# Conv layer: sums beside the taps, one row pipeline up to the output projection, and that projection with rows outermost

## The chip, the cores and the metric

The kernel runs on one core of a Trainium2 chip. The metric is the time of one execution on the device in microseconds, the median of several runs. The engines are TensorE (PE, its weight loads PEld), VectorE (DVE), ScalarE (ACT), GpSimd (POOL) and SyncE (SP), which issues the transfers of the weights.

## What is computed

The kernel is a stack of layers on 512 tokens of 1024 features. The change is in one of them, the conv layer, whose core in the reference is this (E_WIDTH 2048, 31 taps, rows of 64 tokens; the tokens are eight such rows):

```python
def _layernorm(x, g, b):
    xf = x.astype(jnp.float32)
    xc = xf - jnp.mean(xf, axis=-1, keepdims=True)
    var = jnp.mean(xc * xc, axis=-1, keepdims=True)
    return (xc * lax.rsqrt(var + EPS) * g.astype(jnp.float32) + b.astype(jnp.float32)).astype(x.dtype)

def _conv_mixer(h, w_in, b_in, dw, dw_b, ln_g, ln_b, w_out, b_out, conv_fn):
    p = h @ w_in + b_in
    a, gl, gate = jnp.split(p, 3, axis=-1)
    u = a * jax.nn.sigmoid(gl)
    u = conv_fn(u, dw, dw_b)
    u = jax.nn.silu(_layernorm(u, ln_g, ln_b))
    return (u * jax.nn.silu(gate)) @ w_out + b_out
```

The result, times a gate of the modulation, is added to x. All is float32.

## The kernel before

Everything is kept features first: a row is 128 features (on the partitions) by 512 tokens, so the 2048 features of the conv layer are 16 rows, in the tile Y. The program is a list of blocks; at the end of a block all engines meet. Within a block each engine runs its own list in order and they wait on counting semaphores. Weights come as tiles of 2 MB, 128 by 4096, into two slots of K.W; SP issues tile i + 2 when tile i is used up (`prefetch`, line 347).

**Input projection and taps** (`conv_layer`, first block). 12 tiles: 8 of kind G, which hold two value rows (j = 0, 1) and the two rows of their sigmoid gates (j = 2, 3), and 4 of kind Z, the outer gate, in the order GGGZGGZGGZGZ. PE makes four products of eight plain float32 matmuls a tile (line 2884), each into its own bank; tiles alternate between banks 0 to 3 and 4 to 7. ACT applies the sigmoid to j = 2, 3 of a G tile (line 2899) and silu to the four of a Z tile (2905). For each G tile, group g, DVE evacuates the two values (2926), multiplies them with the sigmoids (2932) and then runs 31 taps on each of the two rows (2943, 2947), the two rows in turn, each tap waiting for the one before on its row. Behind the products PE adds up the 16 rows with a matrix of ones (2890), as they come out of the taps.

**Layer norm** (`layer_stats`, second block). DVE takes the mean (2826) and subtracts it from each row (2830), ACT squares (2837), PE sums the squares (2821), ACT makes rstd with Ln and Exp (2840, 2843).

**Scale, silu, gate** (third block). DVE scales 16 rows (2961), ACT applies silu behind it (2974), and then DVE multiplies 16 rows by the outer gate (2966).

**Output projection** (fourth block: `linear_deep`, `Deep`, `Feed`). A float32 product is made of three fp32r products: operands are split into a high part and the rest, and hi*hi, lo*hi and hi*lo are added up. ACT makes high parts of weights (`make_hi`, 518) and rows (`Feed.high`, 396), DVE the rest (527, 406). A weight part is 8 blocks of 128 x 128: one output block j by eight rows. So `split_products` (539) makes 24 matmuls into one bank for each part. Two parts fit in K.parts. The loops are: four tiles, a pair for each half of the outputs (m), the two of a pair (kg) being the two halves of the 16 input rows; in each, four output blocks. All 16 rows are split first, and DVE takes a bank (2788) when its second product is done.

`token_products` (785) in other layers is a product with three matmuls into each of four banks in turn, 24 in all. `Ada.rows` (2057) uses matmuls with 32 columns of weights.

## Time and profile before

| | us |
|---|---|
| median of 3 runs | 4752.32 (4749.88 to 4752.86) |
| profiled execution, its own time | 4745.9 |
| its span | 4743.2 |
| PE busy | 4386.6 (92%) |
| DVE busy | 2499.2 (53%) |
| ACT busy | 1609.2 (34%) |
| granted clock of PE over the span | 0.96 |

The sums below are made against the profiled execution; times in them are microseconds from the start of the span. The conv layer's block with the taps begins at 2732, its output projection ends at 3213. In the timeline a row gives start, length, engine, line, operation and tiles, the number of instructions merged, and in brackets how long the engine was idle before and what ended that. A granted clock of 1.00 is 2.4 GHz, one of 0.5 is 1.2 GHz.

### The profile page before, as it was taken

Reading aid. Unit: us, or ns where it says so; the run is one execution under the profiler, and the core shown is the slowest. Engines: PE = TensorE matmul, PEld = TensorE weight load, DVE = VectorE, ACT = ScalarE, POOL = GpSimd, SP = SyncE. Lnnn points to the kernel's source line nnn. Section 1 sums busy time; section 2 is a strip of 40 time slices with the busy share of each in tenths; the row PEclk is TensorE's granted clock in tenths of the full one; section 3 lists DMA queues with packets and bytes.
Section 4 is the critical chain, followed back from the end, with each engine's and each line's share of the span. In section 5 each row is a group of like instructions: output and inputs, shape, how many; then the busy total and the mean of one; then the engine's idle time right before and its main releaser. Section 6 shows DMA issues by size and latency. Waiting matters only on the chain. (4 is left out here: it accounts for less than half of the span.)

```text
span 4743.2 us, 78502 instructions
## 1 busy us (share of the span) xinstructions
PE 4386.6 (92%) x31788; PEld 3326.4 (70%) x31788; DVE 2499.2 (53%) x4059; ACT 1609.2 (34%) x2467; POOL 320.6 (7%) x307
## 2 busy tenths in 40 slices
PE   8898999999999989999998899978998999999987
PEld 7665787676688767888887644456877567666675
DVE  3635543434445331777777379944534355555563
ACT  2324322323322232666665210133222233334332
POOL 0120000000000000111111000000000022221220
PEclk9889999998999999999999999989998999999998
DMA  3201222221122232111111312111221210000101
GB/s 146 108 19 71 89 98 102 78 82 71 71 89 99 100 129 84 55 59 51 59 54 35 142 55 87 71 54 71 107 98 71 105 37 21 21 20 20 55 3 54
DMA packets 36642, 337.18 MB, mean 71 GB/s; under 512 B 4081, under 2 KB 6385, under 8 KB 18545
## 3 DMA queue, kind: packets, MB, share of 16 engines
q1 hardware_dynamic: 36336, 332.76, 19.0%
q8 instruction: 235, 3.85, 0.3%
q14 instruction: 71, 0.57, 0.0%
HBM read 320.16 MB, written 12.58 MB: 70 GB/s over the span
## 5 line engine op out<-in xcount | busy, mean ns | idle before, releaser
L539 PE MATMUL ps<-hi,weight_parts 128*128 128x512 f32 x5136 | 1610.3, 394 | 121.7 <-DVE lo L406 76.7
L539 PEld LDWEIGHTS ps<-hi,weight_parts 128*128 128x128 f32 x5136 | 979.3, 191 | 341.5 <-issue 123.1
L539 PE MATMUL ps<-lo,weight_parts 128*128 128x512 f32 x2568 | 1011.3, 394 | 0.0
L527 DVE TENSOR_TENSOR weight_parts<-w,weight_parts 128x1024 fp32r<-128x1024 f32 (+1 forms) x336 | 407.0, 1213 | 968.0 <-ACT weight_parts L518 967.8
L518 ACT ACTIVATE weight_parts<-w 128x1024 fp32r<-128x1024 f32 (+1 forms) x336 | 352.0, 1049 | 1200.3 <-PE ps L539 996.5
L539 PEld LDWEIGHTS ps<-lo,weight_parts 128*128 128x128 f32 x2568 | 490.1, 191 | 102.2
L3527 PEld LDWEIGHTS ps<-buffers 64*64 64x64 f32 x12544 | 422.3, 136 | 135.0 <-issue 132.8
L3527 PE MATMUL ps<-buffers 64*64 64x64 f32 x12544 | 450.1, 226 | 61.7 <-issue 33.5
L2409 PE MATMUL ps<-x_parts,column_parts 128*128 128x512 f32 x1536 | 360.6, 392 | 10.4 <-DVE column_parts L2643 9.9
L2884 PE MATMUL ps<-x,w 128*128 128x512 f32 x768 | 331.6, 595 | 6.8 <-PEq L815 6.8
L2409 PEld LDWEIGHTS ps<-x_parts,column_parts 128*128 128x128 f32 x1536 | 286.6, 189 | 69.8 <-DVE column_parts L2643 10.3
L2947 DVE SCALAR_TENSOR_TENSOR buffers<-buffers,vecs 128x392 f32<-128x392 f32 (+14 forms) x480 | 287.0, 716 | 0.0
L2884 PEld LDWEIGHTS ps<-x,w 128*128 128x128 f32 x768 | 146.5, 191 | 191.2 <-issue 191.2
L3520 PE MATMUL ps<-h,w 128*128 128x512 f32 x512 | 228.4, 600 | 1.2 <-PEq L3351 1.2
L3520 PEld LDWEIGHTS ps<-h,w 128*128 128x128 f32 x512 | 96.2, 191 | 117.1 <-issue 115.7
L2434 PE MATMUL ps<-h 128*128 128x128 f32 x1024 | 129.4, 281 | 35.1 <-DVE w L2687 22.6
L2434 PEld LDWEIGHTS ps<-h 128*128 128x128 f32 x1024 | 124.5, 195 | 42.5 <-DVE w L2687 22.2
L3781 ACT ACTIVATE buffers<-ps 128x256 f32<-128x256 f32 x160 | 61.3, 383 | 179.6 <-PE ps L3527 173.9
L3508 POOL TENSOR_TENSOR buffers<-buffers,const 128x512 f32<-128x512 f32 x80 | 101.5, 1269 | 273.9 <-PE ps L3527 204.0
L2643 DVE TENSOR_TENSOR column_parts<-w,column_parts 128x1024 fp32r<-128x1024 f32 x64 | 78.7, 1230 | 58.1 <-ACT column_parts L2515 58.1
L2623 POOL MEMSET w<- 128x1024 f32 x1 | 1.0, 951 | 1539.6 <-POOLq L2130 1539.6
L2409 PE MATMUL ps<-context_parts,column_parts 128*128 128x256 f32 x768 | 104.0, 292 | 0.0
(481 smaller groups left out, 5336.5 us busy)
## 6 DMA issues: line engine op xcount, KB each, us to landing
w<-in_weights SPq DMA_DIRECT2D x126, 2048.0 KB, 8.0
w<-in_wh SPq DMA_DIRECT2D x64, 512.0 KB, 3.6
v_kept<-buffers SPq DMA_DIRECT2D x4, 1024.0 KB, 5.2
buffers<-v_kept SPq DMA_DIRECT2D x16, 256.0 KB, 2.6
h<-x_kept SPq DMA_DIRECT2D x2, 2048.0 KB, 10.4
x<-in_xT SPq DMA_DIRECT2D x4, 512.0 KB, 11.0
x_kept<-h SPq DMA_DIRECT2D x1, 2048.0 KB, 6.9
vc_kept<-x SPq DMA_DIRECT2D x4, 512.0 KB, 2.6
```

The costliest lines, as they stand in the source:

```text
L518: act.activation(K.parts[:, j % 2, 0, 0:nk, :], part_of(K, slot, j, nk, by_row), ACT.Copy)\
L527: dve.tensor_tensor(K.parts[:, j % 2, 1, 0:nk, :], part_of(K, slot, j, nk, by_row), K.parts[:, j % 2, 0, 0:nk, :].bitcast(F32), ALU.subtra ...
L539: mm = pe.matmul(ps, K.parts[:, j % 2, m, k, :], x[:, k * T:(k + 1) * T], start=(first and k == 0 and n == 0), stop=(last and k == nk - 1 ...
L2409: mm = pe.matmul(o, parts[:, half, w, k, :], src[:, m, k, 0:width], start=(k == 0 and n == 0), stop=(k == 7 and n == 2), skip_group_check= ...
L2434: mm = pe.matmul(bank[:, s], l[:, s], r[:, s], start=True, stop=True)
L2643: dve.tensor_tensor(half[:, 1], weight(name), half[:, 0].bitcast(F32), ALU.subtract).then_inc(DL.step(name), 1)
L2884: mm = pe.matmul(bank(i, j), w[:, k, j * P:(j + 1) * P], K.H[:, k, :], start=(k == 0), stop=(k == 7))
L2947: dve.scalar_tensor_tensor(y, u, w, y, ALU.mult, ALU.add).then_inc(K.sem("tapped"), 1)
L3508: pool.tensor_tensor(C, AS, on_chunks(f"{'clow' if d == 0 else 'cup'}{l}"), ALU.mult).then_inc(GM.step(f"c{l}"), 1)
L3520: mm = pe.matmul(K.ps[:, 2 + m % 2, :], w[:, k, m * P:(m + 1) * P], K.H[:, k, :], start=(k == 0), stop=(k == 7))
L3527: mm = pe.matmul(dst[hr(h)], lhsT[hr(h)], rhs[hr(h)], start=start, stop=stop, skip_group_check=True)
L3781: act.activation(in_half(T1, half), bank_half(0, half), ACT.Copy)\
```

## The change

1. The first G tile. PE's order of products in a G tile is 0, 2, 1, 3. For group 0, DVE evacuates value 0, multiplies by gate 0 and runs 19 taps of row 0; only then come value 1, gate 1 and the taps of row 1, in turn with the 12 left of row 0, then 19 of row 1 alone. The other groups are as before: both values, both gates, taps in turn.
2. Sums beside the taps. ACT squares each row as it leaves the taps, into 16 tiles (12 of a new buffer, and sq, ln, rstd): groups 0 to 6 right behind the last sigmoid, group 7 at the end. PE adds up rows and squares, each sum over 32 columns of ones into its own quarter of one bank. The block `layer_stats` is gone.
3. `conv_out` is one block from the sums to the end. Two matmuls over half of the partitions fold the sums to mean and moment; the variance is moment less mean squared, at least 0. Then each row goes through centring, scaling, silu, gating and splitting in turn.
4. The projection (`Outer`) runs over rows outermost: the weights are laid out by rows (`by_rows`), a part is one input row by all eight output blocks, and all eight banks are accumulated at once. The split rows stand in rings of four. A weight part is made when the row two before it is multiplied.

```diff
@@ def tiles_conv(a):
-    return [next(of[kind]) for kind in CONV_TILES] + deep(a["conv_w_out_2"][0])
+    return [next(of[kind]) for kind in CONV_TILES] + by_rows(a["conv_w_out_2"][0])
+class Outer:
+    RING = 4
+    def sync(self, sp):
+        K = self.K
+        prefetch(K, sp, self.nk // 4, lambda g: sp.wait_ge(K.sem("lo_made"), K.count("lo_made", 4 * (g + 1))))
+    def weights_high(self, act, k):
+        K = self.K
+        make_hi(K, act, by_row=True)(k // 4, 0, k // 4, (K.tile + k // 4) % 2, k % 4)
+    def high(self, act, k, row):
+        K = self.K
+        act.wait_ge(K.sem("product"), K.count("product", k - self.RING + 1))
+        act.activation(self.hi[:, k % self.RING, :], row, ACT.Copy).then_inc(K.sem("x_hi"), 1)
+    def low(self, dve, k, row):
+        K = self.K
+        dve.wait_ge(K.sem("x_hi"), K.count("x_hi", k + 1))
+        dve.tensor_tensor(self.lo[:, k % self.RING, :], row, self.hi[:, k % self.RING, :].bitcast(F32), ALU.subtract)\
+           .then_inc(K.sem("x_lo"), 1)
+    def tensor(self, pe, free=None):
+        K = self.K
+        for k in range(self.nk):
+            pe.wait_ge(K.sem("lo_made"), K.count("lo_made", k + 1))
+            pe.wait_ge(K.sem("x_lo"), K.count("x_lo", k + 1))
+            hi, lo = self.hi[:, k % self.RING, :], self.lo[:, k % self.RING, :]
+            for o in range(8):
+                if k == 0 and free is not None:
+                    free(o)
+                for n, (m, x) in enumerate(((0, hi), (0, lo), (1, hi))):
+                    mm = pe.matmul(K.ps[:, o, :], K.parts[:, k % 2, m, o, :], x, start=(k == 0 and n == 0),
+                                   stop=(k == self.nk - 1 and n == 2), skip_group_check=True)
+                if k == self.nk - 1:
+                    mm.then_inc(K.sem("outputs"), 1)
+            if k < self.nk - 1:
+                mm.then_inc(K.sem("product"), 1)
+    def take(self, dve):
+        K = self.K
+        for o in range(8):
+            dve.wait_ge(K.sem("outputs"), K.count("outputs", o + 1))
+            self.add(dve, o // 4, o % 4, K.ps[:, o, :])
@@ def conv_layer(K):
+    order_of = lambda i: (0, 2, 1, 3) if CONV_TILES[i] == "G" else (0, 1, 2, 3)
+    alone = 19
+    first_taps = [(0, n) for n in range(alone)]
+    for n in range(31):
+        first_taps += [(1, n)] + [(0, n + alone)] * (n + alone < 31)
...
-            for k in range(16):
-                pe.wait_ge(K.sem("tapped"), K.count("tapped", 62 * (k // 2) + 61 + k % 2))
-                pe.matmul(sum_bank, K.c("ones"), Y[:, k * T:(k + 1) * T], start=(k == 0), stop=(k == 15))
+            for g in range(8):
+                pe.wait_ge(K.sem("square"), K.count("square", 2 * g + 2))
+                for n, a in enumerate((tile(Y, 2 * g), tile(Y, 2 * g + 1), squares[2 * g], squares[2 * g + 1])):
+                    pe.matmul(sum_bank[32 * n:32 * n + 32], K.c("ones")[:, 0:32], a, start=(g == 0), stop=(g == 7),
+                              skip_group_check=True)
...
+            def square(g):
+                act.wait_ge(K.sem("tapped"), K.count("tapped", 62 * g + 62))
+                for k in (2 * g, 2 * g + 1):
+                    act.activation(squares[k], tile(Y, k), ACT.Square).then_inc(K.sem("square"), 1)
...
+                if i == at[7]:
+                    for g in range(7):
+                        square(g)
+            square(7)
@@ def conv_out(K, Y, Zg, mean, folded, sum_at, add):
+        def _(act):
+            act.activation(folded, K.ps[:, sum_at, :], ACT.Copy).then_inc(K.sem("step_act"), 1)
+            outer.weights_high(act, 0)
+            act.preload_act_table_set(LN_EXP)
+            act.wait_ge(K.sem("mean"), K.count("mean", 1))
+            act.activation(K.sq[:, 0, :], mean, ACT.Square).then_inc(K.sem("moment"), 1)
+            act.wait_ge(K.sem("variance"), K.count("variance", 2))
+            act.activation(K.ln[:, :], K.sq[:, 1, :], ACT.Ln, bias=K.c("eps")).then_inc(K.sem("logged"), 1)
+            act.wait_ge(K.sem("logged"), K.count("logged", 1))
+            act.activation(K.rstd[:, :], K.ln[:, :], ACT.Exp, scale=-0.5).then_inc(K.sem("rstd"), 1)
+            act.preload_act_table(ACT.Silu)
+            outer.weights_high(act, 1)
...
+            silu(0)
+            for k in range(16):
+                if k < 15:
+                    silu(k + 1)
+                act.wait_ge(K.sem("gated"), K.count("gated", k + 1))
+                outer.high(act, k, row(Y, k))
+                if 0 < k < 15:
+                    outer.weights_high(act, k + 1)
...
+            outer.weights_low(dve, 0)
+            dve.wait_ge(K.sem("summed"), K.count("summed", 1))
+            dve.tensor_scalar(mean, mean_ps, 1.0 / count, None, ALU.mult).then_inc(K.sem("mean"), 1)
+            dve.wait_ge(K.sem("mean"), K.count("mean", 1))
+            center(0)
+            dve.wait_ge(K.sem("moment"), K.count("moment", 1))
+            dve.wait_ge(K.sem("summed"), K.count("summed", 2))
+            dve.scalar_tensor_tensor(K.sq[:, 1, :], moment_ps, 1.0 / count, K.sq[:, 0, :], ALU.mult, ALU.subtract)\
+               .then_inc(K.sem("variance"), 1)
+            dve.wait_ge(K.sem("variance"), K.count("variance", 1))
+            dve.tensor_scalar(K.sq[:, 1, :], K.sq[:, 1, :], 0.0, None, ALU.max).then_inc(K.sem("variance"), 1)
+            center(1)
+            dve.wait_ge(K.sem("rstd"), K.count("rstd", 1))
+            scale(0)
+            outer.weights_low(dve, 1)
+            for k in range(16):
+                if k < 15:
+                    scale(k + 1)
+                dve.wait_ge(K.sem("silu"), K.count("silu", k + 1))
+                dve.tensor_tensor(row(Y, k), row(Y, k), row(Zg, k), ALU.mult).then_inc(K.sem("gated"), 1)
+                if k < 14:
+                    center(k + 2)
+                outer.low(dve, k, row(Y, k))
+                if 0 < k < 15:
+                    outer.weights_low(dve, k + 1)
+            outer.take(dve)
```

## Rows read from the trace of the kernel before

**Rows 1.** The page's header: span of the profiled execution.

```profile
span 4743.2 us, 78502 instructions
```

**Rows 2.** Windows: stretch, length, busy PE, PEld, DVE, ACT, POOL, clock, DMA, GB/s.

```profile
2764.00:3074.00 310.00, 310.00 (x724) 137.28 (x723) 309.79 (x522) 29.59 (x37) 0.00 (x0) 1.00 0.21 81
...
3063.50:3077.80 14.30, 14.29 (x34) 6.04 (x32) 11.21 (x20) 0.69 (x1) 0.00 (x0) 1.00 0.39 147
...
3123.00:3128.60 5.60, 5.60 (x13) 4.47 (x14) 5.60 (x9) 5.60 (x11) 0.00 (x0) 0.51 0.00 0
3128.60:3212.95 84.35, 84.31 (x372) 69.44 (x370) 26.21 (x29) 16.41 (x17) 0.00 (x0) 1.00 0.27 100
```

**Rows 3.** Timeline, DVE and ScalarE, first and last group of the taps: start, length.

```profile
2748.23 0.75 DVE L2926 TENSOR_SCALAR buffers<-ps,vecs 128x512 f32<-128x512 f32 x1 [6.12 <-PE ps L2884]
...
2763.29 1.00 DVE L2943 TENSOR_SCALAR buffers<-buffers,vecs 128x512 f32<-128x512 f32 x2
...
3037.35 0.69 DVE L2932 TENSOR_TENSOR buffers<-buffers 128x512 f32<-128x512 f32 x1 [0.21 <-ACT buffers L2899]
...
3038.87 35.84 DVE L2947 SCALAR_TENSOR_TENSOR buffers<-buffers,vecs 128x392 f32<-128x392 f32 x60
...
3036.63 0.69 ACT L2899 ACTIVATE buffers<-ps,vecs 128x512 f32<-128x512 f32 x1 [4.84 <-PE ps L2884]
```

**Rows 4.** Timeline from the last sums to the output projection's end.

```profile
3063.89 13.90 PE L2890 MATMUL ps<-buffers,const 128*128 128x512 f32 x32
...
3078.09 0.69 DVE L2826 TENSOR_SCALAR buffers<-ps 128x512 f32<-128x512 f32 x1 [3.38 <-PEq L2867]
...
3079.54 1.23 ACT L2837 ACTIVATE sq<-buffers 128x512 f32<-128x512 f32 x2 [14.76 <-DVE buffers L2830]
...
3097.19 0.69 ACT L2840 ACTIVATE ln<-ps,const 128x512 f32<-128x512 f32 x1
3097.91 0.63 ACT L2843 ACTIVATE rstd<-ln 128x512 f32<-128x512 f32 x1
3098.79 1.28 ACT L2970 ACT_TABLE_LOAD   x1 [0.26 <-PEq L2816]
3099.15 10.69 DVE L2961 SCALAR_TENSOR_TENSOR buffers<-buffers,vecs,rstd 128x512 f32 x16 [10.62 <-PEq L2816]
3100.09 10.63 ACT L2974 ACTIVATE buffers<-buffers,vecs  x16
3109.76 9.72 DVE L2966 TENSOR_TENSOR buffers<-buffers  x16
...
3122.16 2.49 DVE L406 TENSOR_TENSOR lo<-buffers,hi 128x512 fp32r<-128x512 f32 x4
...
3123.00 0.77 PE L539 MATMUL ps<-hi,weight_parts 128*128 128x512 f32 x1 [25.95 <-DVE lo L406]
...
3212.95 0.75 DVE L2788 SCALAR_TENSOR_TENSOR h<-ps,mod,h 128x512 f32<-128x512 f32 x1 [4.69 <-PE ps L539]
```

**Rows 5.** Timeline of the projection's weight parts, and a chained pair on DVE.

```profile
3131.41 1.06 ACT L518 ACTIVATE weight_parts<-w 128x1024 fp32r<-128x1024 f32 x1 [1.26 <-PE ps L539]
...
3136.85 1.06 ACT L518 ACTIVATE weight_parts<-w 128x1024 fp32r<-128x1024 f32 x1 [4.38 <-PE ps L539]
...
3137.95 1.23 DVE L527 TENSOR_TENSOR weight_parts<-w,weight_parts 128x1024 fp32r<-128x1024 f32 x1 [3.79 <-ACT weight_parts L518]
...
3724.46 0.48 DVE L3334 TENSOR_SCALAR buffers<-buffers,small 128x512 f32<-128x512 f32 x1
...
3724.97 0.75 DVE L3336 SCALAR_TENSOR_TENSOR buffers<-buffers,vecs 128x511 f32<-128x511 f32 x1
```

**Rows 6.** Timeline: 32-column passes (L2057), and ScalarE waiting for L785's products.

```profile
2710.59 3.64 PE L2057 MATMUL ps<-w,ada_in 128*32 128x512 f32 x32 [1.74 <-PEq L2095]
...
3722.22 1.06 ACT L3263 ACTIVATE weight_parts<-w 128x1024 fp32r<-128x1024 f32 x1 [4.38 <-PE ps L785]
...
3727.66 1.06 ACT L3263 ACTIVATE weight_parts<-w 128x1024 fp32r<-128x1024 f32 x1 [4.38 <-PE ps L785]
```

More of the change, by code:

```diff
@@ L2950, in _ @@
                 one(g)
-    K.done(product=48, taken_dve=16, taken_act=16, taken_gate=16, glu=16, tapped=62 * 8, step_dve=1)
+    K.done(product=48, taken_dve=16, taken_act=16, taken_gate=16, glu=16, tapped=62 * 8, step_dve=1, square=16)
     K.tile += 12
-    layer_stats(K, Y, 16, 2048.0, K.c("eps"), K.big(32 * T, T), sum_bank)
-    g, b = K.v("conv_ln_g"), K.v("conv_ln_b")
-    with nc.Block() as block:
+    K.shut()
+    conv_out(K, Y, Zg, tile(U[:, 0, :], 0), tile(U[:, 0, :], 1), sum_at, gated_plus_x(K, m, 0))
@@ new lines, in conv_layer, with conv_out, _, taken @@
+    K.shut()
+    K.shut()
+def conv_out(K, Y, Zg, mean, folded, sum_at, add):
+    nc = K.nc
+    g, b = K.v("conv_ln_g"), K.v("conv_ln_b")
+    row = lambda a, k: a[:, k * T:(k + 1) * T]
+    count = 32 * 2048.0
+    mean_ps, moment_ps = K.ps[:, sum_at + 1, :], K.ps[:, sum_at + 2, :]
+    with Outer(K, 16, add) as outer, nc.Block() as block:
+        @block.sync
+        def _(sp):
+            outer.sync(sp)
+        @block.tensor
+        def _(pe):
+            pe.wait_ge(K.sem("step_act"), K.count("step_act", 1))
+            for half, ps in ((slice(0, 64), mean_ps), (slice(64, 128), moment_ps)):
+                pe.matmul(ps, K.c("ones")[half], folded[half], start=True, stop=True).then_inc(K.sem("summed"), 1)
+            def taken(o):
+                pe.wait_ge(K.sem("variance"), K.count("variance", 1))
+                pe.wait_ge(K.sem("mean"), K.count("mean", 1))
+            outer.tensor(pe, taken)
+        @block.scalar
+        def _(act):
[10 more added lines that the diff above has]
+            outer.weights_high(act, 1)
+            def silu(k):
+                act.wait_ge(K.sem("scaled"), K.count("scaled", k + 1))
+                act.activation(row(Y, k), row(Y, k), ACT.Silu, bias=b[:, k:k + 1]).then_inc(K.sem("silu"), 1)
+            silu(0)
[6 more added lines that the diff above has]
+                    outer.weights_high(act, k + 1)
@@ L2969, in _, with center @@
-        def _(act):
-            act.preload_act_table(ACT.Silu)
-            with act.Fori(0, 16) as i:
-                at = Y[:, ds(i * T, T)]
-                act.wait_ge(K.sem("scaled"), K.count("scaled", i + 1))
-                act.activation(at, at, ACT.Silu, bias=b[:, ds(i, 1)]).then_inc(K.sem("silu"), 1)
-    K.done(scaled=16, silu=16)
-    K.shut()
-    with Parts(K, 16) as (hi, lo):
-        linear_deep(K, hi, lo, 8, gated_plus_x(K, m, 0), feed=Feed(K, tiles_of(Y, 16), hi, lo))
-    K.shut()
+            def center(k):
+                dve.tensor_tensor(row(Y, k), row(Y, k), mean, ALU.subtract).then_inc(K.sem("centered"), 1)
@@ L2982, in sgu_layer @@
+            outer.take(dve)
+        outer.done()
+    K.done(step_act=1, summed=2, mean=1, moment=1, variance=2, logged=1, rstd=1, silu=16, scaled=16, gated=16, centered=16)
 def sgu_layer(K):
```

113 lines of the change are left out of this document (57 added, 56 removed).

## Prediction

> **What bounds the kernel now.** The page gives the span [rows 1] and shows TensorE busy nearly everywhere, so I did not read it for a bound of the whole. I looked up the lines of the conv layer in the timeline and cut its 480 us into stretches. Three stretches have different limits.
>
> First the taps: in 310 us both PE and DVE are busy throughout [rows 2]. Which of the two sets the end is settled by one row: for group 7, the last one, DVE has evacuated its values and then waits 0.21 us for the last sigmoid, which ScalarE started at 3036.63 behind a product of PE [rows 3]. PE's input projection runs without a gap at 6.87 us for a product of eight matmuls (DVE, which waits for each, starts at 2748.23 after a wait of 6.12 behind its 0.75). So PE's 44th product starts the last group of taps, and then DVE needs 35.8 us.
>
> Second, from the last tap (3038.87 + 35.84 = 3074.71) to the first product of the output projection (3123.00): 48.3 us in which one pass over 16 rows follows the next: sums, mean and centring, squares and their sums, rstd, scaling with silu, gating, and only then the split [rows 4]. PE is nearly idle for 25 of them. This is the stretch that the change attacks.
>
> Third, the output projection: 384 matmuls, the first 5.6 us at a granted clock of 0.51, the rest at 1.00 [rows 2], the last bank taken at 3212.95 [rows 4]. It takes 89.95 us from first matmul to last take; a product of 24 matmuls takes 5.44 us (3131.41 to 3136.85) [rows 5]. PE sets the pace there.
>
> **Part 1, the first tile reordered.** In the new order (value 0, gate 0, value 1, gate 1) the sigmoid of channel block 0 can follow the second product, done at 2748.2, rather than the third [rows 3]. With the table load (1.28), the sigmoid and the multiply (0.69 each) the first tap would start at about 2750.9 instead of 2763.3, 12.4 us earlier. Against that, 19 taps of block 0 and later 19 of block 1 run alone, each waiting for the one before. Now 60 taps take 35.84 us, 0.60 each, because two chains alternate; a chained instruction starts about 0.04 us behind the end of the other (3724.46 + 0.48 to 3724.97) [rows 5]. At a middle length of 0.72 us, my estimate from the neighbouring 0.75 us row, that is some 0.75 each: 38 x 0.15 = 6 us. So DVE ends group 0 about 6 us earlier. But what is late next? The last group still cannot start its taps before the sigmoid that ends at 3037.32, since both gates precede the taps there and the fourth product of a tile stays the fourth. The lead is spent in that wait: it grows from 0.21 to about 6 us. PE's pace depends on none of this, as the banks of tile 0 are wanted back only when tile 2 starts, four products behind 2761.8, at about 2789. I count 0.2 us at most, take 0, and keep the full 6 us as a rival.
>
> **Part 2, sums beside the taps.** The 16 squares move to ScalarE. Fourteen run behind the last sigmoid (from 3037.3, 14 x 0.6 = 8.6 us, as two take 1.23 [rows 4]), ahead of the last four gates, whose first product PE ends one product of 6.87 us behind the sigmoid's, at 3043.5. That delays the first gates by 2 to 3 us, and nobody waits for these. Only the last two squares are exposed: 0.03 + 1.2 us behind the last tap, 3075.95. PE then does four sums of 32 columns side by side. The nearest row is the 128*32 group, 32 passes in 3.64 us, 0.11 each [rows 6]: eight passes 0.9 us, or 1.8 at half clock, plus about 0.3 of start and drain. PE has been idle for 6 us by then (28 of 32 sums are done from 3063.5 on in some 6 us); behind its longer gap today it starts at half clock [rows 2], so I lean to that end. Today PE's 16 full sums take 13.9 us [rows 4] and end at 3077.79, and the block's end costs 0.30 to 3078.09. New: block end at 3077.5 to 3078.4, I take 3078.2. Part 2 alone saves nothing here; its worth is that the pass of squares in the block that follows, from 3079.54 to the Ln at 3097.19, disappears.
>
> **Part 3, from the sums to the first product.** I lay the written order out from that block end, with the durations of [rows 4] and [rows 5] and 0.03 to 0.04 us for a handoff. ScalarE copies the sum (0.69), splits weights (1.06): 1.69. DVE's low half (1.15 until the next may start) lies in front of the mean: 2.88; this covers PE's two small sums. Mean 0.69: 3.60. Square of it 0.63: 4.26. Variance 0.75: 5.04. Clamp 0.48: 5.55. Ln 0.69: 6.27. Exp 0.63: 6.93. Silu's table 1.28: 8.24. Second weight part 1.06 on ScalarE: 9.3, and 1.15 on DVE: 10.45. Scaling of row 1 (0.67 until the next): 11.12. Gate of row 0, 0.69: 11.8. Its high part, behind silu of row 1: 12.5. Low part 0.69: 13.2. PE 0.15 later (low part ends 3122.85, PE at 3123.00): 13.4. So PE starts at 3078.2 + 13.4 = 3091.6 instead of 3123.00: 31.4 us. The bounds: 2 us less if the moment sum lies hidden and PE is at full clock, 3 us more if each of the 15 steps costs 0.2 us of handoff.
>
> The table load is on that chain once. In the trace 1.28 us are followed by the activation 0.02 us later [rows 4]. The Trainium skill, page "ScalarE: Activation LUTs", section "What ACT_TABLE_LOAD costs", counts a drain of about 1.38 us beside each load; by it the start would be some 1.4 us later, and the rows here don't show it.
>
> **Part 4, rows outermost.** The matmuls are as many and of the same form; PE's 89.95 us stay if it is fed. Eight banks are accumulated at once and the bank changes every three matmuls. The nearest rows are those of L785, where the bank changes every three matmuls too: ScalarE, which waits for its products of 24, starts at 3722.22 and 3727.66, 5.44 us apart as well [rows 6]. What is new is that in each row the work of the feeding engines hangs on PE: weight part k+1 may be made only when row k-1 has been multiplied, and ScalarE and DVE, both in order, have silu, scaling, gating and centring queued behind it. From the start of a row on PE: ScalarE starts 0.19 later and ends 1.25, low half 1.29 to 2.44, scaling ends 3.19, silu lets the next start at 3.88, high part 4.50, low part 5.23, PE could go on at 5.38. Against 5.44: it holds, by 0.06 us. DVE's own load is 0.67 + 3 x 0.61 + 1.15 = 3.65 us a row (16 in 10.69, 16 in 9.72). I take 0.4 us in all for a few late rows; the bounds are 0 and, at 0.1 us more for each of five handoffs, 0.44 x 14 = 6 us.
>
> At the end all eight banks come in the last row, 0.68 us apart; DVE's take has 0.75 us but lets the next start after 0.67, so the last take stands where it stood. The norm behind it and everything later only move.
>
> **The sum.** 31.4 - 0.4 = 31.0 us. Against the profiled execution: span 4743.2 to 4712.2, its own time 4745.9 to 4714.9. The median of the runs stands 6.4 above that time, so 4752.3 - 31.0 = 4721.3.
>
> **The rivals.** (a) The row is not fed in 5.44 us. For it: the margin is 0.06 us of a chain of eight links. Against: every link was taken with its measured length. At 5.8 us a row the time is 4721.3 + 5.5, about 4727. (b) The end is exposed: DVE comes late to the last row and the eight takes (8 x 0.67 = 5.4, less 0.7) stand behind PE, 4726. DVE's 3.65 of 5.44 us speak against it. (c) Part 1's lead survives, by 6 us: 4715. The 0.21 us wait of group 7 speaks against it. (d) The slower side: the small gaps between rows and the change of bank every three matmuls keep the granted clock at half. A row then takes 24 x 0.43 = 10.2 us, 4.8 more; it decides from 6.5 rows at half clock on (31 / 4.8), and all 16 give 77 - 3 (already slow today) - 31 = 43 slower, 4795. Against it: L785 with its bank change [rows 6], and the clock back at 1.00 5.6 us into the projection [rows 2]. The Trainium skill, page "TensorE: Matmul & The Clock Gate", section "A second HAM failure mode: psum-queue depth-cycling", describes a kernel in which cycling through PSUM banks left small idle times often enough for the clock to swing between its levels; that rule would give case (d), and the trace's nearest line does not bear it out. (e) Little or nothing comes of it, within 0.2%, because a wait that I read wrongly puts 22 us or more back.
>
> **How the numbers follow.** Forecast 0.66, (a) 0.20, (b) 0.05, (c) 0.04, (d) 0.02, (e) 0.03. Faster by over 0.2% (9.5 us, about what a measurement of this kernel can tell from no change): 0.95; within: 0.03; slower: 0.02. Range: below, 4721.3 less 2 of the start, less part of (c) and 2 of scatter (the three runs span 3 us): 4715. Above: the start 3 later, (a) with 6, 3 of scatter: 4733.
>
> **What would show it.** The first group-7 tap at about 3038 as before, with a wait of DVE of several us ahead of gate 1 in groups 5 and 7; the first matmul of the projection 16 to 18 us behind the last tap; ScalarE's weight parts 5.44 us apart; a granted clock of 1.00 from the second row on; the last take about 90 us behind the first matmul. A first tap of group 7 before 3037 would make part 1 wrong; weight parts over 5.5 us apart part 4.

## The result and the profile after

The changed kernel takes 4722.52 us (4715.32 to 4724.4, four runs) against 4752.59 for the kernel before beside it: a ratio of 0.9934 (95% interval 0.9917 to 0.9951), 30 us. Five more runs of the unchanged file later gave 4727.4 and 0.9947 (0.9934 to 0.9961), 25 us. The profiled pair lies closer together: the header of the page of the changed kernel is

```profile
span 4720.5 us, 78323 instructions
```

22.7 us under [rows 1]. So I cut both spans at the same instructions: at the start of the conv layer's block (DVE's first instruction in it), the end of the last take, and the first and last y_sum of the wkv layer, a later layer of many small products.

| stretch (us of each profile) | before | after | gain |
|---|---|---|---|
| start of the conv layer's block | 2732.21 | 2732.00 | 0.2 |
| from there to the last take of the output projection | 481.49 | 449.23 | 32.3 |
| from there to the first sum (y_sum) of the wkv layer | 681.86 | 680.35 | 1.5 |
| first to last sum of the wkv layer | 743.24 | 755.47 | -12.2 |
| from there to the end of the span | 104.40 | 103.45 | 0.9 |

The conv layer gained more than the 31.0 us of the forecast, and a layer that the change doesn't touch gave part of it back. I follow the gain first, by the steps of the prediction.

**Part 1, DVE around the first group and the last.** Timeline of the changed kernel, DVE (columns as in the rows of before), which answers to [rows 3]:

```profile
2750.92 0.55 DVE L3018 TENSOR_SCALAR buffers<-buffers,vecs 128x512 f32<-128x512 f32 x1
2751.50 13.10 DVE L3022 SCALAR_TENSOR_TENSOR buffers<-buffers,vecs 128x392 f32<-128x392 f32 x18
...
2954.86 0.69 DVE L2998 TENSOR_TENSOR buffers<-buffers 128x512 f32<-128x512 f32 x1 [2.39 <-ACT buffers L2956]
...
3037.26 0.69 DVE L2998 TENSOR_TENSOR buffers<-buffers 128x512 f32<-128x512 f32 x1 [3.92 <-ACT buffers L2956]
```

The taps begin at 2750.9, where the forecast had them (times here are from the start of the span, as in the rows of before). Eighteen taps alone take 13.10 / 18 = 0.73 us each (0.75 was estimated). The lead that is left is waited off in groups 5 and 7, 2.39 + 3.92 = 6.3 us, both times for a sigmoid; the last tap ends at 3074.63, against 3074.71 before.

**Part 2 and the first half of part 3.** Timeline from there to the row chain; the wait in brackets of the row at 3075.86 is PE's:

```profile
3074.66 0.63 ACT L2970 ACTIVATE ln<-buffers 128x512 f32<-128x512 f32 x1 [9.97 <-DVE buffers L3022]
3075.20 0.61 ACT L2970 ACTIVATE rstd<-buffers 128x512 f32<-128x512 f32 x1
3075.86 1.07 PE L2947 MATMUL ps<-buffers,const 128*32 128x512 f32 x2 [5.75 <-ACT rstd L2970]
...
3078.10 0.60 ACT L3063 ACTIVATE buffers<-ps 128x512 f32<-128x512 f32 x1 [2.29 <-PEq L2923]
3078.59 1.05 ACT L523 ACTIVATE weight_parts<-w 128x1024 fp32r<-128x1024 f32 x1
...
3080.86 0.69 DVE L3098 TENSOR_SCALAR buffers<-ps 128x512 f32<-128x512 f32 x1
3081.59 0.63 ACT L3067 ACTIVATE sq<-buffers 128x512 f32<-128x512 f32 x1 [0.64 <-DVE buffers L3098]
...
3082.97 0.43 DVE L3106 TENSOR_SCALAR sq<-sq 128x512 f32<-128x512 f32 x1
...
3083.44 0.72 ACT L3069 ACTIVATE ln<-sq,const 128x512 f32<-128x512 f32 x1 [1.22 <-DVE sq L3106]
3084.19 0.63 ACT L3071 ACTIVATE rstd<-ln 128x512 f32<-128x512 f32 x1
3084.84 1.28 ACT L3072 ACT_TABLE_LOAD   x1
3086.13 1.06 ACT L523 ACTIVATE weight_parts<-w 128x1024 fp32r<-128x1024 f32 x1
...
3087.22 1.22 DVE L532 TENSOR_TENSOR weight_parts<-w,weight_parts 128x1024 fp32r<-128x1024 f32 x1 [1.61 <-ACT weight_parts L523]
3088.36 0.74 DVE L3094 SCALAR_TENSOR_TENSOR buffers<-buffers,vecs,rstd 128x512 f32<-128x512 f32 x1
...
3090.42 0.69 DVE L758 TENSOR_TENSOR ring_lo<-buffers,ring_hi 128x512 fp32r<-128x512 f32 x1
...
3091.21 0.77 PE L771 MATMUL ps<-ring_hi,weight_parts 128*128 128x512 f32 x1 [10.38 <-DVE ring_lo L758]
```

The squares of rows 14 and 15 are all that stands behind the last tap; the new block begins at 3078.10. What [rows 4] showed as passes over 16 rows is a chain of single rows here, and PE's first product starts at 3091.21 instead of 3123.00.

**Part 4, the projection.** Windows of the changed kernel (columns as in [rows 2]): the gap with the chain, the first 3 us of the projection, the rest of it.

```profile
3084.00:3093.00 9.00, 1.79 (x4) 1.49 (x5) 6.40 (x10) 6.18 (x9) 0.00 (x0) 0.50 0.00 0
...
3092.00:3095.00 3.00, 3.00 (x9) 2.33 (x9) 1.67 (x3) 1.05 (x2) 0.00 (x0) 0.60 0.00 0
3095.00:3181.00 86.00, 85.44 (x376) 69.12 (x374) 56.40 (x75) 31.68 (x41) 0.00 (x0) 1.00 0.26 98
```

And the last take, from DVE's timeline, with two of the weight parts made on the way:

```profile
3099.62 1.23 DVE L532 TENSOR_TENSOR weight_parts<-w,weight_parts 128x1024 fp32r<-128x1024 f32 x1 [5.85 <-ACT weight_parts L523]
3105.06 1.22 DVE L532 TENSOR_TENSOR weight_parts<-w,weight_parts 128x1024 fp32r<-128x1024 f32 x1 [1.55 <-ACT weight_parts L523]
...
3175.72 5.51 DVE L2869 SCALAR_TENSOR_TENSOR h<-ps,mod,h 128x512 f32<-128x512 f32 x8 [1.81 <-PE ps L771]
```

PE is busy for 85.44 of 86 us at a granted clock of 1.00. The fourteen weight parts that DVE makes during this projection, from 3099.62 to 3170.69, are 71.07 / 13 = 5.47 us apart. First matmul to end of the last take is 3181.23 - 3091.21 = 90.0 us. In the kernel before the same measure gives 3212.95 + 0.75 - 3123.00 = 90.7; the forecast's 89.95 ran to the start of the last take. So the projection became 0.7 us shorter. The clock of 0.60 over the window from 3092 to 3095 puts its return to 1.00 at about 3094.4, 3.2 us behind the first matmul, where [rows 2] has it 5.6 us behind. Matmuls start 0.43 us apart at the slow level (3091.77 and 3092.20 in PE's timeline) instead of 5.44 / 24 = 0.23, so that is worth about 1.1 us, and the late rows cost 13 x 0.03 = 0.4.

**What is given back.** The group of the wkv layer's small products, from the groups of the page of the changed kernel (busy time, mean of one in ns, idle time ahead of it and what ended most of that), and PE's first two waits in the wkv layer, from the view of waits:

```profile
L3671 PE MATMUL ps<-buffers 64*64 64x64 f32 x12544 | 450.8, 226 | 70.6 <-issue 41.5
```

```profile
PE ps L3671 <- issue: 43.3, 49, 4.3
PE ps L3671 <- ACT buffers L3862: 8.9, 22, 0.4
```

The same two views of the kernel before:

```profile
L3527 PE MATMUL ps<-buffers 64*64 64x64 f32 x12544 | 450.1, 226 | 61.7 <-issue 33.5
```

```profile
PE ps L3527 <- issue: 35.7, 48, 4.3
PE ps L3527 <- ACT buffers L3718: 9.3, 22, 0.7
```

The work is the same, 12544 matmuls of 226 ns, and so are the waits for ScalarE. What grew by 7.6 us is time in which PE waited for nothing that the profile shows. It is not the whole of the 12.2 us: in this profile PE is also busy for 3.5 us more in that layer, at a granted clock of 0.96 instead of 0.97. In the second profile of the changed kernel (e0_same, below) busy time and clock are those of before, and the time for "issue" alone is 11.6 us more. This idle time needed experiments of its own.

### The profile page after: what moved, and what is told of

The parts are those of the page before. It is cut to its first block and busy times, and to the rows that moved or that the text cites. A ratio compares the mean times of both kernels' runs of the same rounds, so it can differ in the third digit from the quotient of the medians.

```text
span 4720.5 us, 78323 instructions
## 1 busy us (share of the span) xinstructions
PE 4369.1 (93%) x31792; PEld 3315.4 (70%) x31792; DVE 2506.9 (53%) x4061; ACT 1609.5 (34%) x2469; POOL 320.5 (7%) x307
## 3 DMA queue, kind: packets, MB, share of 16 engines
q8 instruction: 235, 3.85, 0.3%
## 5 line engine op out<-in xcount | busy, mean ns | idle before, releaser
L544 PE MATMUL ps<-hi,weight_parts 128*128 128x512 f32 x4880 | 1527.9, 394 | 95.6 <-DVE lo L411 50.4
L544 PEld LDWEIGHTS ps<-hi,weight_parts 128*128 128x128 f32 x4880 | 929.2, 190 | 304.0 <-issue 96.1
L544 PE MATMUL ps<-lo,weight_parts 128*128 128x512 f32 x2440 | 959.8, 393 | 0.0
L544 PEld LDWEIGHTS ps<-lo,weight_parts 128*128 128x128 f32 x2440 | 464.9, 191 | 96.6
L2515 PEld LDWEIGHTS ps<-h 128*128 128x128 f32 x1024 | 124.5, 195 | 42.4 <-DVE w L2768 22.0
```

What stands on the lines that cost most here:

```text
L544: mm = pe.matmul(ps, K.parts[:, j % 2, m, k, :], x[:, k * T:(k + 1) * T], start=(first and k == 0 and n == 0), stop=(last and k == nk - 1 ...
L2515: mm = pe.matmul(bank[:, s], l[:, s], r[:, s], start=True, stop=True)
```

## The experiments

All lengths by stretch are measured as in the table above, "conv" from the start of the conv layer's block to the last take, "wkv" from its first to its last sum. "Issue" is PE's idle time for "issue" in the wkv layer, all lines together.

| kernel | time (range, runs), us | ratio to before (95%) | conv | wkv | issue |
|---|---|---|---|---|---|
| before | 4752.59 (4749.88 to 4754.67, 4) | 1 | 481.5 | 743.2 | 43.0 |
| p6_before_again | 4750.67 (4745.98 to 4755.15, 10) | 1.0007 (0.9997 to 1.0017) | 481.6 | 744.0 | 43.5 |
| after | 4722.52 (4715.32 to 4724.4, 4) | 0.9934 (0.9917 to 0.9951) | 449.2 | 755.5 | 50.7 |
| e0_same | 4727.4 (4721.32 to 4731.38, 5) | 0.9947 (0.9934 to 0.9961) | 449.1 | 755.9 | 54.6 |
| e1_first_tile_back | 4723.36 (4720.69 to 4731.46, 5) | 0.9946 (0.9932 to 0.996) | 449.2 | 752.9 | 50.7 |
| e2_last_tile_early | 4716.14 (4713.14 to 4727.09, 5) | 0.9926 (0.9912 to 0.9939) | 445.2 | 763.2 | 61.4 |
| e3_sums_only | 4746.61 (4740.65 to 4752.97, 11) | 0.9992 (0.9983 to 1.0001) | 475.2 | 746.0 | 45.0 |
| e5_both | 4717.57 (4713.9 to 4720.36, 5) | 0.9936 (0.9923 to 0.995) | 442.5 | 750.8 | 48.6 |
| e6_extra_pass | 4726.55 (4720.74 to 4730.48, 4) | 0.995 (0.9935 to 0.9966) | 455.1 | 752.0 | 48.6 |
| p1_before_pad12 | 4748.94 (4744.66 to 4753.28, 11) | 1.0001 (0.9992 to 1.001) | 481.6 | 742.0 | 39.5 |
| p2_after_pad244 | 4728.47 (4720.69 to 4731.48, 5) | 0.996 (0.9946 to 0.9974) | 455.1 | 739.9 | 39.9 |
| p3_before_pad244 | 4745.6 (4736.61 to 4747.16, 10) | 0.9987 (0.9977 to 0.9997) | 486.3 | 735.1 | 36.0 |
| p4_both_pad244 | 4732.39 (4729.74 to 4738.27, 5) | 0.9962 (0.9948 to 0.9977) | 443.5 | 745.5 | 42.4 |
| p5_both_pad94 | 4705.68 (4704.48 to 4711.0, 4) | 0.9914 (0.9897 to 0.993) | 443.0 | 740.6 | 42.3 |

The runs of one kernel lie up to 16 us apart, while conv repeats within some 0.1 us between two profiles of one kernel (481.49 and 481.57, 449.23 and 449.11). So small terms are read from the stretches and not from the medians. The stretches, though, are those of one profiled execution a kernel. For e2_last_tile_early that is the slowest of its five runs (4727.09, 11 us above the median), for p2_after_pad244 the fastest of its five (4720.69, 7.8 below the median); their wkv lengths are to be read with that in mind.

**The same kernel once more (e0_same).**

> The changed kernel again, without an edit. Question: between the last take of the conv layer's projection and the end of the span the profiled execution of the changed kernel needed 1539.3 us (4720.5 - 3181.2), that of before 1529.5 (4743.2 - 3213.7), 9.8 more, and the wkv layer, from its first to its last sum, 755.5 us against 743.2, 12 more, although nothing of it was edited. Theory 'place': the program's new length moves the code of that layer and PE waits longer for instructions, always: wkv 755 us again, within 2, in this profile, and a ratio of 0.993 to 0.995 to before. Theory 'scatter': that layer's time scatters from run to run by several us whatever the kernel: wkv anywhere from 742 to 757 us here, and the runs of one kernel differ by up to 10 us.

Conv 449.1, wkv 755.9. The stretches behind the start of the conv layer repeat within 1 us, the wkv layer within 0.5: its loss isn't an accident of one run.

**The first tile's order undone (e1_first_tile_back).**

```diff
-    order_of = lambda i: (0, 2, 1, 3) if CONV_TILES[i] == "G" else (0, 1, 2, 3)
+    order_of = lambda i: (0, 1, 2, 3)
...
-    taps_of = lambda g: first_taps if g == 0 else [(j, n) for n in range(31) for j in (0, 1)]
+    taps_of = lambda g: [(j, n) for n in range(31) for j in (0, 1)]
...
```

> The changed kernel with the first G tile as before: products in the order 0, 1, 2, 3, values and gates ahead of the taps in group 0 too, taps in turn. Theory of the prediction (the last group's taps start behind PE's 44th product): last tap within 0.3 us of the changed kernel's 3074.6, first product of the projection at 3091.2 within 0.5, time the same within 0.1%; DVE's wait ahead of gate 1 of group 7 falls from 3.9 to about 0.2 us. Rival (the lead of 6 us survives in the changed kernel): last tap 4 to 6 us later and the kernel 0.1% slower.

Conv is 449.2 in both. With the old order the wait ahead of group 7 is small again, as this row of DVE's timeline of e1_first_tile_back shows:

```profile
3040.86 0.69 DVE L2998 TENSOR_TENSOR buffers<-buffers 128x512 f32<-128x512 f32 x1 [0.22 <-ACT buffers L2956]
```

So part 1 of the change is worth nothing by itself: it turns a wait at the start into one of the same length at the end.

**The last G tile one place earlier (e2_last_tile_early).** If the sigmoid of group 7 is what holds DVE, its tile must come sooner. The Z tile ahead of it changes places with it.

```diff
-CONV_TILES = "GGGZGGZGGZGZ"
+CONV_TILES = "GGGZGGZGGGZZ"
-    sum_bank = bank(at[7], 0)
+    sum_bank = bank(10, 0)
...
             pe.wait_ge(K.sem("taken_dve"), K.count("taken_dve", 16))
+            pe.wait_ge(K.sem("taken_gate"), K.count("taken_gate", 12))
```

> The changed kernel with the last G tile moved one place ahead (GGGZGGZGGGZZ), and the sums in the bank of the tile before last. If PE's product sets the start of the last group of taps, the group starts when group 6 ends, at 3031.3, and its gates wait for nothing: DVE gives back 3.9 us of wait, the last tap ends at about 3070.7, the first product of the projection starts at about 3087.3, and the kernel is 4 us faster than the changed one (ratio to before about 0.0008 lower). Rival (PE, behind its last product at 3063.5 and 28 sums, becomes the limit, or ScalarE's squares, which now hold back eight gates, do): less than 2 us.

Conv falls by 4.0 us to 445.2; the last tap ends 338.5 us behind the start of the block instead of 342.6. DVE's waits during the taps, in the view of waits, first of the changed kernel, then of e2_last_tile_early (us in total, times, longest):

```profile
DVE buffers L2998 <- ACT buffers L2956: 14.5, 3, 8.2
DVE buffers L2991 <- PE ps L2940: 9.1, 1, 9.1
```

```profile
DVE buffers L2999 <- ACT buffers L2957: 10.6, 2, 8.2
DVE buffers L2992 <- PE ps L2940: 9.0, 1, 9.0
```

The third wait for a sigmoid, 3.9 us, is gone, and that is the gain at the taps. It shows that this wait, and not DVE, set the end of the taps in the changed kernel. Two smaller terms cancel behind it. The last sums run at the full clock here (0.62 us each instead of 1.07), so the first product starts 354.2 us behind the start of the block instead of 359.2, 5.0 sooner. The projection then takes 91.0 us instead of 90.0, as its clock comes back later, 4.6 us behind the first matmul (PE's window in e2_last_tile_early, with the clock behind the busy times):

```profile
3087.60:3092.00 4.40, 4.39 (x10) 3.45 (x11) 2.47 (x4) 1.24 (x2) 0.00 (x0) 0.50 0.00 0
```

The median falls too, to 4716.14, though the wkv layer takes 763.2 in the profile. As that profile is the slowest run, and none of its other stretches is long, the wkv layer was most likely shorter in the other four.

**The sums alone (e3_sums_only).** The sums beside the taps stay; behind them stand the old passes over 16 rows and the old projection.

```diff
-    return [next(of[kind]) for kind in CONV_TILES] + by_rows(a["conv_w_out_2"][0])
+    return [next(of[kind]) for kind in CONV_TILES] + deep(a["conv_w_out_2"][0])
...
+    with Parts(K, 16) as (hi, lo):
+        linear_deep(K, hi, lo, 8, gated_plus_x(K, m, 0), feed=Feed(K, tiles_of(Y, 16), hi, lo))
...
+            for k in range(1, 16):
+                center(k)
...
+            with dve.Fori(0, 16) as i:
+                at = Y[:, ds(i * T, T)]
+                dve.scalar_tensor_tensor(at, at, g[:, ds(i, 1)], K.rstd[:, :], ALU.mult, ALU.mult)\
+                   .then_inc(K.sem("scaled"), 1)
```

> Part 2 alone with the old passes: sums beside the taps and mean and rstd as in the changed kernel, but all 16 rows are centred, then scaled with silu, then gated, then split, and the projection goes over output blocks as before. Expected from the durations: rstd and centring end 13.5 us behind the sums' block end (3078.1) instead of 20.5 in the kernel before, so the first product starts at about 3115.5 to 3116.5 and the kernel gains 7 us on before (ratio 0.9985); the other 24 us of the gain then belong to the row pipeline with rows outermost. Rival (the squares' pass was most of the gain): 15 us or more here.

Conv 475.2, 6.3 us less than before, of the 32.3 of the whole. The other 26.0 come from the row chain with rows outermost, which e3 doesn't take apart. DVE's timeline of e3_sums_only shows the three passes over the rows still there:

```profile
3086.25 9.11 DVE L3068 TENSOR_TENSOR buffers<-buffers 128x512 f32<-128x512 f32 x15
3096.00 10.69 DVE L3088 SCALAR_TENSOR_TENSOR buffers<-buffers,vecs,rstd 128x512 f32 x16 [0.65 <-PEq L3047]
3106.61 9.72 DVE L3093 TENSOR_TENSOR buffers<-buffers  x16
```

**Last tile early and the second weight part early (e5_both).** Beside the edit of e2, the second weight part is made inside the chain of the variance, where both engines wait, instead of behind the table load.

```diff
             act.activation(K.sq[:, 0, :], mean, ACT.Square).then_inc(K.sem("moment"), 1)
+            outer.weights_high(act, 1)
...
             act.preload_act_table(ACT.Silu)
-            outer.weights_high(act, 1)
...
             center(1)
+            outer.weights_low(dve, 1)
             dve.wait_ge(K.sem("rstd"), K.count("rstd", 1))
             scale(0)
-            outer.weights_low(dve, 1)
```

> The changed kernel with the last G tile one place ahead (as in e2_last_tile_early) and with the second weight part moved ahead: ScalarE makes its high half behind the square of the mean, DVE its low half behind the second centring, ahead of rstd, where they waited 1.2 and 0.9 us. Theory (the chain from the last tap to the first product is bound by these two engines' lists, as laid out in the prediction): the first product starts 2.0 to 2.4 us sooner behind the last tap (14.3 us instead of 16.6), and with the tile 6 us sooner than in the changed kernel; time 6 us below it. Rival (the weight part now holds back Ln or the scaling by as much): first product within 0.7 us of 16.6 behind the last tap.

Conv 442.5, another 2.7 us below e2. In the timeline of e5_both ScalarE's half of the part ends ahead of rstd and DVE's begins ahead of it, and PE starts at 3086.37, 11.0 us behind the block's first copy at 3075.40. In the changed kernel it was 3091.21 - 3078.10 = 13.1.

```profile
3079.42 1.04 ACT L523 ACTIVATE weight_parts<-w 128x1024 fp32r<-128x1024 f32 x1
...
3081.22 1.22 DVE L532 TENSOR_TENSOR weight_parts<-w,weight_parts 128x1024 fp32r<-128x1024 f32 x1
3081.49 0.63 ACT L3073 ACTIVATE rstd<-ln 128x512 f32<-128x512 f32 x1
...
3086.37 0.77 PE L771 MATMUL ps<-ring_hi,weight_parts 128*128 128x512 f32 x1 [8.24 <-DVE ring_lo L758]
```

**One more DVE pass in each row (e6_extra_pass).** How tight is the row chain?

```diff
                     scale(k + 1)
+                dve.tensor_tensor(K.sq[:, 0, :], mean, mean, ALU.subtract)
                 dve.wait_ge(K.sem("silu"), K.count("silu", k + 1))
```

> The changed kernel with one more pass of DVE in each row of the pipeline (a subtraction of the mean from itself into a spare tile, between scaling and gating), 0.61 us a row. In the changed kernel ScalarE's weight parts are 5.47 us apart on average, where 24 matmuls take 5.44. Theory (the chain from one row's product over weight part, scaling, gate and split to the next row closes at 5.4 us, with no slack): the rows come about 6.05 us apart, 13 rows x 0.58 = 7.5 us later at the last take. Rival (PE alone sets the pace and DVE, busy 3.65 us of 5.44, has 1.8 us to spare): rows stay at 5.45 to 5.5 us, and nothing changes.

Conv 455.1, 5.9 us more: 0.6 ahead of the first product, and in the projection 95.4 us (3097.12 to 3192.56) instead of 90.0. ScalarE's weight parts in the timeline of e6_extra_pass:

```profile
3105.72 1.06 ACT L523 ACTIVATE weight_parts<-w 128x1024 fp32r<-128x1024 f32 x1 [6.17 <-PE ps L771]
3111.16 1.06 ACT L523 ACTIVATE weight_parts<-w 128x1024 fp32r<-128x1024 f32 x1 [0.58 <-PE ps L771]
3117.24 1.06 ACT L523 ACTIVATE weight_parts<-w 128x1024 fp32r<-128x1024 f32 x1 [1.22 <-PE ps L771]
```

They lie 5.44 and 6.08 us apart, in turn. So a longer chain does reach PE, as the small margin of part 4 says, but every second row only: 5.74 us a row on the mean (3105.72 to 3180.36, 13 steps), where 6.05 were expected. DVE's load is no limit here: 3.65 + 0.61 us a row. What holds is a chain, and why it is late only every second time I haven't isolated.

**Where the program lies.** The wkv layer's issue gaps sit in its dense stretches, one behind another. For the changed kernel the windows from the end of one gap to the begin of the next, in four places, are:

```profile
3949.45:3954.39 4.94, 3.71 (x120) 3.63 (x121) 2.41 (x6) 0.99 (x3) 1.27 (x1) 1.00 0.02 3
3954.40:3958.96 4.56, 3.71 (x121) 3.57 (x120) 2.83 (x7) 0.99 (x3) 2.34 (x3) 1.00 0.02 4
3999.43:4004.33 4.90, 3.72 (x120) 3.63 (x121) 2.79 (x7) 0.99 (x3) 1.27 (x1) 1.00 0.01 3
4004.34:4009.13 4.79, 3.77 (x122) 3.63 (x121) 2.79 (x7) 0.61 (x2) 1.28 (x1) 1.00 0.02 3
```

Each window holds 120 to 122 matmuls and as many weight loads: 241 to 243 together. The gaps at their ends are 1.2 and 0.9 us (PE's timeline of the changed kernel):

```profile
3954.40 0.80 PE L3671 MATMUL ps<-buffers 64*64 64x64 f32 x21 [1.23 <-issue]
3958.97 0.50 PE L3671 MATMUL ps<-buffers 64*64 64x64 f32 x10 [0.85 <-issue]
```

```profile
q8 instruction: 235, 3.85, 0.3%
```

```profile
q8 instruction: 1, 0.02, 1.7%
```

A packet is 16.4 KB (3.85 MB for 235), and there is one between two gaps. By their times in the trace, the four gaps at 3949.45, 3954.40, 3999.43 and 4004.34 end 1.25, 1.47, 1.25 and 1.43 us after such a packet has landed. Over the whole wkv layer 110 or 111 of these packets arrive in every one of the fourteen traces. "Issue" gaps of over 0.5 us are 32 in the kernel before, 39 in the changed one and 26 in p3; all but one or two in each trace end within 2 us after a packet of their own has landed, most of them 1.2 to 1.7 us after it. So what differs between the kernels is not how often the program is fetched but how many of the fetches leave PE idle. What decides that for a packet I haven't isolated.

The Trainium skill, page "Runtime: NRT & Kernel Launch", section "Instruction fetch mechanics", says that instructions are fetched in 16 KiB blocks of 256. The trace agrees with the size, and the distance fits with some waits and branches that the windows don't count. It also says that fetching is mostly hidden because issue is slower than the fetch; with matmuls that start some 0.04 us apart (4.94 us for 120) the rows here don't agree.

If so, the length may depend on where the program lies, and a kernel can be moved without changing its work. The pads are waits on a count that is reached long before:

```diff
+            for _ in range(20):
+                pe.wait_ge(K.sem("product"), K.count("product", 0))
```

In p1 they are 20, and the compiled list of PE is then as long as that of the changed kernel, 12 instructions more than before; in p3 they are 486, and the page of the run counts 244 instructions more than that of before (78746 against 78502). Both stand in the pass with silu, where PE is idle. In p2 (186 in the normalization ahead of the conv layer, 300 in the first block of the output projection), p4 (486 in that normalization) and p5 (186 there) the changed kernel (p2) or e5_both (p4, p5) is padded, which moves PE's list by 244, 244 and 94.

> The kernel before with 20 waits that are already met on PE's queue in its idle block ahead of the output projection; in the compiled program PE's list is then 43974 instructions long, as in the changed kernel, instead of 43962, so that all that follows on PE stands 12 places later. No work is changed. So far the wkv layer took 743.2 us in the profile of before (PE idle for 'issue' 38.3 us in it), 746.0 (42.4) with a list of 43970, and 752.9 to 763.2 (44.8 to 55.2) in four profiles with 43974. Theory 'place' (the position of PE's code decides how long it waits for instructions in that layer's loop): wkv about 750 to 758 us here, issue idle 45 or more, and the kernel 7 to 10 us slower than before (ratio 1.0015 to 1.002). Rival (another effect of the changed conv layer, or scatter): 743 to 747 us and a ratio of 1.000, within 0.0005. The Trainium skill, page 'Runtime: NRT & Kernel Launch', section 'Instruction fetch mechanics', says that instructions are refilled in blocks of 256 and that a taken branch breaks the sequential prefetch; by that rule the place within a block would matter.

> The changed kernel with 244 more instructions on PE's list ahead of that layer (486 waits already met, in two stretches in which PE is idle anyway: behind the norm ahead of the taps and behind the two small sums of conv_out). PE's list is 44218 long, 256 more than in the kernel before. They may show as up to 12 us each on PE in gaps of 7 and 10 us, so up to 6 us can come on the path of the conv layer; that part is read off and set aside. Theory 'place' with a period of 256: the wkv layer takes 741 to 747 us again, issue idle about 38, 9 us less than in the changed kernel. Rival (the period is another, or not the place): 752 to 758 us as in the changed kernel.

> The kernel before with 486 waits that are already met on TensorE while VectorE multiplies the rows (TensorE has nothing else there), so the program behind them is moved as it is in p2, but nothing of the computation changes. Theory 'place' (how long TensorE waits for its own instructions in the wkv layer follows from where its program lies): the wkv layer, first to last sum, which took 742 to 746 us with the output projection of before, moves by several us, to below 738 or above 750, and the run with it. Theory 'projection' (it follows from which of the two projections the kernel has): 742 to 746 us, and the whole within 0.1% of the kernel before.

> e5_both (the changed kernel with the last tile early and the second weight part early) and 486 met waits on TensorE in the normalization ahead of the convolution's products, where TensorE waits anyway. Cost of the waits: conv starts up to 6 us later, since the same number cost about that in p2. Theory 'place': the wkv layer falls to about 740 us as in p2 with the same shift, from 751 in e5_both, and the time is about 4717.6 + 6 - 11 = 4713. Theory 'noise' (a kernel's runs differ by as much on their own): the wkv layer is anywhere between 740 and 763 us, and the time about 4717.6 + 6 = 4723.

> The kernel before, unchanged, profiled a second time, to see how far one and the same program's wkv layer differs between two profiles. The changed kernel's two profiles gave 755.5 and 755.9 us. If the length belongs to the program: 742 to 745 us here (743.2 in the first profile). If it belongs to the run: anywhere from 735 to 760 us. The time as a whole is that of the kernel before, within 0.1%.

> e5_both with 186 met waits on TensorE in the normalization, a number that cost the start of the convolution about 1 us in p2, so the program behind is moved by about 94 instructions. If the length of the wkv layer follows from where the program lies, it differs from the 750.8 us of e5_both by several us in either direction, and the run with it: 4717.6 + 1, less or plus that. If the length goes by the output projection alone: 751 us, and 4718.5 in all.

With p1 the idea seemed to fall: 742.0, as before. But moved by 244, the kernel before loses 8.1 us of its wkv layer and the changed one 15.6, and e5_both 10.2 by 94 and 5.3 by 244. Two profiles of one program differ by 0.8 (before and p6) and 0.5 us (after and e0). The waits view of p3_before_pad244 gives the same line as above:

```profile
PE ps L3532 <- issue: 28.7, 39, 4.3
PE ps L3532 <- ACT buffers L3723: 9.3, 22, 0.7
```

The time for "issue" went from 35.7 to 28.7 while the other waits stayed. So met waits far ahead of this layer can move its length.

How far that holds, the run times say. The waits cost time of their own in the conv layer, 4.8 us in p3 and 5.8 in p2. The median of p3 is still 6.0 us below that of before beside it, and the runs of p5 (4704.48 to 4711.0) all lie below those of e5_both (4713.9 to 4720.36). For these two the shorter layer shows in the runs too. In p2 it doesn't: with 15.6 us less in the wkv layer and 5.8 more in the conv layer its median would be some 10 us below that of the changed kernel, and it is 4728.47 against 4722.52 and 4727.4. Its profile was its fastest run. So a part of this layer's length also changes from run to run of one build, and how much wasn't measured: only two kernels were profiled twice.

Nor does PE's position alone tell the length: p1 and the changed kernel have lists of the same length on PE and differ by 13.5 us. The lists of the other engines differ between them too (the pages count 4059 and 4061 instructions on DVE, 2467 and 2469 on ScalarE), and I didn't try these.

p5 is the best kernel here, 4705.68: conv 443.0 and wkv 740.6. p4, with 486 waits, loses 19 us ahead of the conv layer, where up to 6 were expected: PE's idle time ahead of its first product is 25.75 us instead of 6.80 in e5_both, since so many waits are no longer covered there.

## Why the prediction was right, and what it left out

By time it was right: 4722.52 and 4727.4 against 4721.3, inside 4715 to 4733. By its steps:

- **Part 1** was right, with its wait: 0 was counted, and e1 shows 0. Its sum put the lead of about 6 us into the wait of the last group alone, its list of signs into groups 5 and 7; it is 3.92 us in group 7 and 2.39 in group 5.
- **Part 2** was right: block end 3078.10 against 3078.2. Behind the last tap stand two squares (1.15 us) and two rounds of four sums side by side, 0.85 us apart; PE did start at the slow level.
- **Part 3** was right: 13.1 us against 13.4. The handoffs cost 0.03 to 0.04 us as taken; the copy and the first weight part let the next start a little sooner. The next activation starts 0.01 us behind the table load (3084.84 + 1.28 to 3086.13). So the drain of about 1.38 us that the Trainium skill, page "ScalarE: Activation LUTs", section "What ACT_TABLE_LOAD costs", counts beside a load is not in this trace either.
- **Part 4** was right in its mechanism: PE sets the pace, rows 5.47 us apart, and the 0.03 us a row beyond 5.44 make the 0.4 us that were set aside. What it left out is the half clock, which it took over from before and which lasted 3.2 us instead of 5.6. With it the projection became 0.7 us shorter instead of 0.4 longer. Rival (b) didn't come: DVE waited 1.81 us for PE ahead of the eight takes. Rival (a) didn't come, but e6 shows how near it was: 0.61 us more in the chain costs 0.27 us a row.
- **Rival (d)**, the slower side, had its condition: PE cycles through eight banks, three matmuls each. The clock stays at 1.00 for 86 us. The case that the Trainium skill describes, page "TensorE: Matmul & The Clock Gate", section "A second HAM failure mode: psum-queue depth-cycling", is one of small idle times between groups of matmuls; the trace doesn't agree with a swing of the clock here, and of such idle time it has 0.56 us in 86.
- **Rival (c)**, the lead that survives, needed e2's order of tiles: 4.0 of the 6 us then appear.

The sum has one step that failed: "the norm behind it and everything later only move". The conv layer gave 32.3 us instead of 31.0 (31.6 up to the first product and 0.7 in the projection, against 31.4 and -0.4), and behind it 9.8 us were given back in the profiled pair (12.2 in the wkv layer, less 2.5 elsewhere). By the medians the gain is 30 us in the first comparison and 25 in the second, between the profiles 23: the first is near 31.0, but a part of that is the scatter of the runs. 31 less 5 to 10 us would have been the better sum. What the trace of before had to say on it was the idle time for "issue" in that layer, 43 us that I didn't look at because the change doesn't touch it. That the time still lies in the range is in part luck: the upper side was set aside for a late start and rival (a), not for this. Its direction and size could not be told from that trace.

## What to carry to other kernels

When a chain of passes over all rows stands between two busy stretches of PE, turn it into a chain of single rows that feeds PE as it goes: here 26 of 32 us came from that, and only 6 from moving the sums beside other work. A lead won at the start of a pipeline is worth something only if the last item is released sooner too; look at the wait ahead of the last group before the first is reordered. And read a change's gain by stretches cut at the same instructions: a dense loop elsewhere can be 10 us shorter or longer for another build with the same work. Take more than one profile of each, and see whether the profiled run is a typical one.

## What the runs showed of the hardware

- PE stood idle for 0.7 to 1.3 us about every 5 us in places of the densest layer, mostly after 240 to 250 matmuls and weight loads and 1.2 to 1.7 us after a packet of 16.4 KB had landed on the queue for instructions. Over the wkv layer the idle time for "issue" is 36 to 61 us of 735 to 763. With 186 or more met waits on PE, several hundred us ahead of the layer, the profiles show it 5 to 16 us shorter.
- On DVE a step of a chain takes 0.73 us when the chain runs alone (13.10 us for 18), and 0.60 when two chains alternate (35.84 for 60).
- A met wait on PE costs about 0.05 us: with 186 of them ahead of the conv layer (p5) PE's idle time there is 9.55 us, with 486 (p4) 25.75, so 16.2 us for 300.
- PE went back to the full clock 3.2 us into the projection in the changed kernel and 4.6 us into it in e2_last_tile_early, each time after a gap of 10.38 us, and 5.6 us into it before the change, after one of 25.95 [rows 2]. The gap alone doesn't tell it.
